# Weight lows, root and splits in another order at two feed-forward entries, and the last tile last in the first unit of two mixers

## What is computed

```
for layer in range(2):
    g = norm_gains[layer]
    x = x + 0.5 * _swiglu(_rmsnorm(x, g[0]), w_gate[layer, 0], w_up[layer, 0], w_down[layer, 0])
    h = _rmsnorm(x, g[1])
    mix = _conv_rwkv_mixer(h, ...) if layer % 2 == 0 else _mla_mixer(h, ...)
    x = x + mix
    x = x + 0.5 * _swiglu(_rmsnorm(x, g[2]), w_gate[layer, 1], w_up[layer, 1], w_down[layer, 1])
_swiglu: (silu(h @ w_gate) * (h @ w_up)) @ w_down      # widths 1024 -> 2816 -> 1024
```

## Time and profile before

| | us |
|---|---|
| median of 3 runs (lowest, highest) | 2406.77 (2405.48, 2410.96) |
| profiled execution | 2409.44 |
| its span on the core | 2407.6 |
| PE busy | 2340.6 |
| DVE busy | 1725.3 |
| ACT busy | 1139.8 |
| POOL busy | 879.3 |

### The profile page before, as it was taken

How to read it: one execution, slowest core, us unless ns; L and a number is a source line. 1 busy time by engine, 2 the same in 40 slices (tenths; PEclk the granted TensorE clock), 3 DMA queues, 4 the chain that set the end, 5 groups by cost and what they waited for, 6 DMA issues and landing times.

```text
span 2407.6 us, 42060 instructions
## 1 busy us (share of the span) xinstructions
PE 2340.6 (97%) x16891; PEld 1984.7 (82%) x16891; DVE 1725.3 (72%) x2282; ACT 1139.8 (47%) x1746; POOL 879.3 (37%) x533
## 2 busy tenths in 40 slices
PE   8999989999999999988999999999999999999999
PEld 6667768789899787876898997998997557898997
DVE  6999986497486489865883867865855776883871
ACT  5533353465265336334652654643643344662552
POOL 3799944332313456522114123123134211114123
PEclk9999999999999999999999999999999999999999
DMA  5222214233333432002334333342334121233333
GB/s 152 79 79 79 75 57 120 82 88 91 111 107 94 117 88 77 27 3 59 105 100 120 94 107 90 106 119 83 106 93 108 48 64 53 83 100 107 106 89 96
DMA packets 420789, 214.46 MB, mean 89 GB/s; under 512 B 17317, under 2 KB 419035, under 8 KB 420603
## 3 DMA queue, kind: packets, MB, share of 16 engines
q1 hardware_dynamic: 416523, 209.05, 30.5%
q10 hardware_dynamic: 4080, 2.83, 0.5%
HBM read 209.22 MB, written 2.10 MB: 88 GB/s over the span
## 4 chain that ended last, share of the span: by engine, by line
PE 75%; DVE 12%; POOL 7%; issue 3%; ACT 2%; DMA 0%; ACTq 0%; POOLq 0%; DVEq 0%
PE bank L982 10%; PE bank L988 10%; PE bank L1000 10%; PE bank L341 10%; PE bank L344 10%; PE bank L337 10%; POOL w_lo L319 3%; PE bank L1866 2%; PE bank L1863 2%; PE bank L1859 2%; DVE bank L1693 1%; DVE gu_w_lo L592 1%; PE bank L3405 1%; PE bank L2751 1%; POOL tmp L1321 1%
## 5 line engine op out<-in xcount | busy, mean ns | idle before, releaser
L319 POOL TENSOR_TENSOR w_lo<-w_raw,w_hi 128x1024 fp32r<-128x1024 f32 (+5 forms) x276 | 532.8, 1932 | 611.8 <-ACT w_hi L311 610.0
L311 ACT ACTIVATE w_hi<-w_raw 128x1024 fp32r<-128x1024 f32 (+5 forms) x276 | 237.6, 861 | 626.1 <-PE bank L344 472.5
L592 DVE TENSOR_TENSOR gu_w_lo<-gu_w,gu_w_hi 128x1024 fp32r<-128x1024 f32 (+1 forms) x254 | 363.1, 1432 | 99.7 <-ACT gu_w_hi L583 99.0
L664 POOL TENSOR_TENSOR ffn_aL<-tmp,ffn_aH 128x512 fp32r<-128x512 f32 x88 | 132.5, 1505 | 728.6 <-ACT ffn_aH L708 728.6
L583 ACT ACTIVATE gu_w_hi<-gu_w 128x1024 fp32r<-128x1024 f32 (+1 forms) x254 | 299.7, 1183 | 4.3 <-DVE gu_w L566 3.0
L982 PE MATMUL bank<-hH,gu_w_hi 128*128 128x256 f32 x1248 | 300.2, 280 | 0.7 <-ACT tmp L700 0.7
L988 PE MATMUL bank<-hL,gu_w_hi 128*128 128x256 f32 x1248 | 299.0, 279 | 0.0
L982 PEld LDWEIGHTS bank<-hH,gu_w_hi 128*128 128x128 f32 x1248 | 231.6, 188 | 2.0 <-ACT tmp L700 1.4
L988 PEld LDWEIGHTS bank<-hL,gu_w_hi 128*128 128x128 f32 x1248 | 231.1, 188 | 0.1
L982 PE MATMUL bank<-st_hi,gu_w_hi 128*128 128x256 f32 x936 | 225.9, 280 | 1.5 <-ACT tmp L700 1.5
L988 PE MATMUL bank<-st_lo,gu_w_hi 128*128 128x256 f32 x936 | 225.5, 279 | 0.0
(11 more groups left out here) (553 smaller groups left out, 4712.9 us busy)
## 6 DMA issues: line engine op xcount, KB each, us to landing
gu_w<-in_ffn_w_gate SPq DMA_DIRECT2D x88, 512.0 KB, 3.7
gu_w<-in_ffn_w_up SPq DMA_DIRECT2D x88, 512.0 KB, 4.8
w_raw<-in_w_in SPq DMA_DIRECT2D x48, 512.0 KB, 3.8
w_raw<-in_ffn_w_down SPq DMA_DIRECT2D x64, 384.0 KB, 3.5
w_raw<-in_ffn_w_down SPq DMA_DIRECT2D x64, 320.0 KB, 3.2
w_raw<-in_even_w_in SPq DMA_DIRECT2D x26, 512.0 KB, 3.9
w_raw<-in_w_conv_out SPq DMA_DIRECT2D x8, 512.0 KB, 3.8
w_raw<-in_w_out SPq DMA_DIRECT2D x8, 512.0 KB, 3.8
```

Of the source, the lines that this page charges most:

```text
L311: nc.scalar.activation(w_hi[u % 2][:, 0:K, :], w_raw[u % 4][:, 0:K, :], ACT.Identity).then_inc(w_hi_ready, 1)
L319: nc.gpsimd.tensor_tensor(w_lo[u % 2][:, 0:K, :], w_raw[u % 4][:, 0:K, :], w_hi[u % 2][:, 0:K, :].bitcast(F32), ALU.subtract).then_inc(w_l ...
L592: nc.vector.tensor_tensor(gu_wl[v % 3][:, b0:b1, :, :], gu_w[v % 3][:, b0:b1, :, :], gu_wh[v % 2][:, b0:b1, :, :].bitcast(F32), ALU.subtra ...
L664: nc.gpsimd.tensor_tensor(aL[:, in_half(n), :], up_t[:, :], aH[:, in_half(n), :].bitcast(F32), ALU.subtract).then_inc(a_lo, 1)
```

## The change

Four edits go together.

1. The first unit of both mixers is made by a new function, `unit_last_tile_late`: the passes are `w_hi` by `hH`, `w_lo` by `hH`, `w_hi` by `hL`, each over tiles 0 to 6, and the three matmuls of tile 7 come after them.
2. In blocks 2 and 3 VectorE makes the two lows of weight unit 1 (`gu_lo`) right after the update of tile 7, at the end of the stage before, ahead of the low part and the square sum of that tile; in the feed-forward's own list they fall away.
3. In blocks 2 and 3 ScalarE makes the root ahead of `turned_high_act`, and all three splits of the next unit's weights ahead of `silu` and `high`.
4. In all four blocks the one-column Ln of L736 is replaced by a load of the table set `natural_log_exp_and_others`.

```diff
+        def unit_last_tile_late(pe, u, K, q):
+            g = G_OF[u]
+            pe.wait_ge(w_hi_ready, u + 1)
+            pe.wait_ge(group_read, g - 3)
+            out, H, L = bank[g % 4][:, :], w_hi[u % 2], w_lo[u % 2]
+            for k in range(K - 1):
+                pe.wait_ge(h_hi, DT * q + k + 1)
+                nc.tensor.matmul(out, H[:, k, :], hH[:, k, :], start=k == 0, stop=False)
+            pe.wait_ge(w_lo_ready, u + 1)
+            for k in range(K - 1):
+                nc.tensor.matmul(out, L[:, k, :], hH[:, k, :], start=False, stop=False)
+            for k in range(K - 1):
+                pe.wait_ge(h_lo, DT * q + k + 1)
+                nc.tensor.matmul(out, H[:, k, :], hL[:, k, :], start=False, stop=False)
+            pe.wait_ge(h_hi, DT * q + K)
+            nc.tensor.matmul(out, H[:, K - 1, :], hH[:, K - 1, :], start=False, stop=False)
+            nc.tensor.matmul(out, L[:, K - 1, :], hH[:, K - 1, :], start=False, stop=False)
+            pe.wait_ge(h_lo, DT * q + K)
+            nc.tensor.matmul(out, H[:, K - 1, :], hL[:, K - 1, :], start=False, stop=True).then_inc(unit_done, 1)
...
 # ffn_act
                         if v == 0:
-                            s.activation(small[:, 7:8], small[:, 0:1], ACT.Ln).then_inc(act_step, 1)
-                            act_sent(act_step)
+                            s.preload_act_table_set("natural_log_exp_and_others")
                         if v == 0 and e:
                             state_high_act(act, e, 3)
                         if v == 0 and e >= 2:
+                            inverse_root()
                             turned_high_act(act, e)
                             continue
                         if v == 1 and e >= 2:
-                            inverse_root()
                             gu_hi(act, n + 1, 0)
                             gu_hi(act, n + 1, 1)
+                            gu_hi(act, n + 1, 2)
                             silu(n - 1)
                             high(n - 1)
-                            gu_hi(act, n + 1, 2)
                             continue
...
 # ffn_dve
-                            if e or v_:
+                            if e == 1 or e == 0 and v_:
                                 gu_lo(v, n + 1, 0)
                                 gu_lo(v, n + 1, 1)
...
 # ffn_dve, after the update of tile j, for the next block of the same list
+                        elif j == 7 and c == 1:
+                            gu_lo(v, n0 + GU + 1, 0)
+                            gu_lo(v, n0 + GU + 1, 1)
...
 # odd_dve, after the loop over the tiles
+            gu_lo(v, 3 * GU_UNITS + 1, 0)
+            gu_lo(v, 3 * GU_UNITS + 1, 1)
             turned_tile(DT - 1)
...
 # even_pe
-            for n_ in range(2):
-                unit(pe, U_EI + n_, 8, hH, hL, ready=(h_lo, DT * q) if n_ == 0 else None)
+            unit_last_tile_late(pe, U_EI, 8, q)
+            unit(pe, U_EI + 1, 8, hH, hL)
             norm_pe(pe)
...
 # odd_pe
-                unit(pe, U_OI + n_, 8, hH, hL, ready=(h_lo, DT * q) if n_ == 0 else None)
                 if n_ == 0:
+                    unit_last_tile_late(pe, U_OI, 8, q)
                     norm_pe(pe)
-                elif n_ == 3:
+                else:
+                    unit(pe, U_OI + n_, 8, hH, hL)
+                if n_ == 3:
```

## The result

The changed kernel takes 2393.94 us (median of 5 runs, 2393.07 to 2396.92), the kernel before 2406.77 us in the same session: a ratio of 0.9946, 95% interval 0.9935 to 0.9956. A second round of the same kernel gave 0.9948 (0.9934 to 0.9961). The forecast was 2392.0 in a range of 2388.5 to 2400.0, and faster with 0.9.

A forecast was written before the change was run, and what follows sets the result against it. TensorE, busy 97% of the span, was taken as the bound. Mixers 8.2, third entry 4.1, fourth 2.1 and first 0.4 sum to 14.8 us, from 2406.8 to 2392.0 us; range 2388.5 to 2400.

The forecast's parts named there:

- Mixers, 8.2 forecast: Entries of even and odd mixer: wait for tile 7 of `hH` and half clock behind it both go, 4.1 us each.
- The lower bound of 2.07: Each mixer entry: gain in us if only the wait goes and the slow clock's cost stays.
- The 9.59 us of the prediction: Even mixer, first unit's start to second's: 5.44 of work, 2.07 of waiting, about 2.1 of half clock and restart.
- Third entry, 4.1 forecast: Third feed-forward entry (e = 2): earlier lows save 4.70 us up to the first product, less 0.6; bounds 2.3 and 4.7.
- the 0.6 that was taken off: Third feed-forward entry: a stop or so for `tmp` behind the first product, inherited once the front is relieved, costing 0.6 us.
- the distance of tile 7 from the front: Third entry: tile 7 is updated 1.9 us nearer to TensorE's front than in the fourth, leaving 0.4 of 2.3 us.
- Fourth entry, 2.1 forecast: Fourth feed-forward entry: fewer `tmp` stops; ScalarE 1.5 us earlier, VectorE's sums 0.8, 2.3 in all; 2.1 taken, bounds 0 and 2.4.
- First entry, 0.4 forecast: First feed-forward entry: preload nearly without effect on the 1.6 us stop, the chain being VectorE's own; bounds -0.5 and 2.0.
- Second entry, 0 forecast: Second feed-forward entry: only the preload differs and nothing waits for the root, so no gain.
- No mixer gain was lost: Rival: VectorE's stretch or a late odd square sum loses one mixer's 4.1 us; 2396.1; 0.27 jointly with entries moving little.
- The table change does nothing: Rival: Ln loads its old set again, one more 1.28 us load at each entry; 2394.1 us; chance 0.04.
- the added table set makes loads slower: Rival: one set more makes some loads fetches from memory, 2.4 us more each; 2416 us with ten; chance 0.03.

The follow-up runs named there:

- lows only: Kernel before with only VectorE's two lows of weight unit 1 moved earlier, at third and fourth feed-forward entry; ratio 0.9983.
- all but the order: The whole change without ScalarE's new order at third and fourth entry; ratio 0.9957.
- mixers only: Kernel before with only the new first unit of both mixers (eighth tile last in all passes); ratio 0.9975.
- order alone: Kernel before with only ScalarE's new order at third and fourth entry; one profiled run, 8.32 us from first to seventh product at the fourth.
- the two dosed units: Kernel before with two, or five, matmuls of L by hH ahead of the eighth of H by hH in both mixers' first unit; ratios 0.9988 and 0.9981.
- after again: The whole changed kernel once more, unaltered, for a second profile; ratio 0.9948.

## Why the prediction was right, step by step

- **Mixers, 8.2 forecast.** 7.97 in the profiled pair, by the order of events that was forecast: `w_lo` and tile 6 in time, no wait, the clock kept, the odd sum in time. What was missing is that the half clock is not certain; by the records it went with where in time the stop lay. By the twelve stops the mean gain is (10 x 3.98 + 2 x 2.37) / 12 = 3.7 us a place, 7.4 in all; 2.37 (8.27 less 5.90, odd mixer of lows only) is what stop and restart alone cost. The lower bound of 2.07 left the restart's 0.3 out. The 9.59 us of the prediction mixed two views (chain and timeline); by the timeline it is 9.43.
- **Third entry, 4.1 forecast.** 4.78 measured. The 4.70 up to the first product are there; the 0.6 that was taken off for stops inherited behind it did not come. ScalarE's new order is what prevents them: without it 1.86 us come back (all but the order), and without the preload too 3.09 (lows only). The size was off, and the ground for it, the distance of tile 7 from the front, did not bind. VectorE's block moved to the weight sums as forecast (L588 at 1499.31 takes 2.23 us, the next one like it 0.69), and hides there. The 4.70 itself was one of several outcomes at this entry. Over its six profiles with late lows and the old order it takes 30.17 to 30.64 us from front to seventh product, mean 30.3; so the mean gain is 4.5. In mixers only both stops came and the clock stayed (20.63), and 9.58 followed. A stop less up front is given back behind the first product, since VectorE and ScalarE are as late as before.
- **Fourth entry, 2.1 forecast.** 2.44. It is at the upper bound, all three stops gone. The step that split the gain into 1.5 for ScalarE and 0.8 for VectorE failed: they don't add, ScalarE's order alone is enough (8.32 in order alone, as after).
- **First entry, 0.4 forecast.** 0.55 at the stop, 0.6 over the entry, by the preload alone. The ground given (near nothing, since the chain is VectorE's own work) was half wrong: the load does reach it. By which link was not tried.
- **Second entry, 0 forecast.** Its stop is 0.37 us before and after.
- **Sum.** 14.8 forecast. With the mean gains 7.4 + 4.5 + 2.4 + 0.6 it is 14.9. That the two agree so well is in part luck: the mixers were taken 0.8 too high, the entries 0.9 too low. In the profiled pair these places gave 15.9 (7.97 + 4.78 + 2.44 + 0.71), with 2.0 lost in stretches that the change doesn't touch. The timed interval, 10.6 to 15.6, holds 14.8 and 14.9. The median of the five runs came out 2 us above the forecast, and no run settles why; the pauses in the 64x64 stretch (2.9 us between the shortest and the longest of the twelve profiles without the two dosed units) and the first block (2.2 us) are wider than that.
- **Rivals.** No mixer gain was lost (mixers only). "The table change does nothing" is nearly right within the whole change, where it is worth 0.6, and wrong by itself, where it has 1.9. That the added table set makes loads slower didn't show: they still take 1283 ns each in the profile after.

Left open: whether the place of a stop alone decides on the half clock, as the twelve cases suggest, what the pauses called "issue" are, what decides between VectorE and GpSimd at the third entry, and which of ScalarE's two moves the fourth entry needs.

## What to carry to other kernels

Where an accumulation waits for its last operand, do everything that does not need it first, in all passes: the wait and the clock behind it went together in both mixers, and in the four cases tried, covering a fifth to a half of the stop of 2.07 us was enough to keep the clock. Look at what comes next before a stop is removed: the lows alone gained 4.7 us and lost 3.0 again, and only the order on the other engine kept them. One trace's stop may be one of two outcomes: where VectorE and GpSimd run beside each other (2.35 or 4.02 us for the same two instructions) or the clock hangs on a stop, read the sum over the stretch in several profiles and not the stop.

## What the runs showed of the hardware that was not expected

- Equal stops of 2.07 us at the same instruction were followed by the half clock in ten of twelve cases, stops of 1.62 and 0.94 us there in none of four. In the 64x64 stretch a pause of 1.77 or 1.78 us at one instruction was followed by it in two profiles (after again, 0.50 from about 1035 us on, and all but the order) and not in five, with shorter pauses ahead of it in all. Behind the ten stops the fall came 0.07 to 1.52 us after TensorE had resumed, while it was busy. The Trainium skill (TensorE: Matmul & The Clock Gate, on the HAM clock gate) says that the moment of a transition varies from run to run; equal stops with different outcomes agree with that, and so does the raster of instants that begins elsewhere in each profile.
- A restart costs 0.3 us beyond the stop without any change of clock: 0.29 behind a stop of 1.62 us (7.35 - 5.44 - 1.62), 0.33 behind one of 0.94.
- The same two instructions on VectorE took 2.35 or 4.0 us from run to run of the same code, by whether GpSimd's subtraction or VectorE's won the second place; TensorE's wait moved by 1.6 us (two stops, 0.97 and 1.61, or the first alone), the end of the stretch by 0.5 (30.64 or 30.17).
- A table load took 1283 ns in every group, before and after. The Trainium skill (ScalarE: Activation LUTs, on what ACT_TABLE_LOAD costs) has about 1283 ns for the load, which agrees, and 2.66 us with a drain; here the activation starts right behind the load (at 1509.65 + 1.28 and 1510.95 in the third entry of before), so no drain of that size stands beside it.
